# A hybrid decoder step on Trainium2: two of four expert rows fetched whole, row weights ahead of the dots, rows 3 and 2 added first on TensorE

## The reference

```python
def peer_ffn(x, w_pq, sub_keys, u_tab, v_tab):
    B, T, D = x.shape
    nt = B * T
    nb = -(-nt // PEER_BLOCK)
    xf = jnp.pad(x.reshape(nt, D), ((0, nb * PEER_BLOCK - nt), (0, 0))).reshape(nb, PEER_BLOCK, D)

    def one(xb):
        q = (xb @ w_pq).reshape(PEER_BLOCK, PEER_HEADS, 2, PEER_QDIM // 2)
        s = jnp.einsum('phcd,hckd->phck', q, sub_keys).astype(jnp.float32)
        ts, ti = lax.top_k(s, PEER_TOPK)
        cand = ts[:, :, 0, :, None] + ts[:, :, 1, None, :]
        cidx = ti[:, :, 0, :, None] * N_KEYS + ti[:, :, 1, None, :]
        fs, fpos = lax.top_k(cand.reshape(PEER_BLOCK, PEER_HEADS, -1), PEER_TOPK)
        eidx = jnp.take_along_axis(cidx.reshape(PEER_BLOCK, PEER_HEADS, -1), fpos, axis=-1)
        g = jax.nn.softmax(fs, axis=-1)
        u = u_tab[eidx]
        v = v_tab[eidx]
        a = jax.nn.gelu(jnp.einsum('pd,phkd->phk', xb, u).astype(jnp.float32), approximate=False)
        return jnp.einsum('phk,phkd->pd', (g * a).astype(v.dtype), v)

    y = lax.map(one, xf)
    return y.reshape(nb * PEER_BLOCK, D)[:nt].reshape(B, T, D)

def block_tail(x, mix, w_out, ln_g, ln_b, w_pq, sub_keys, u_tab, v_tab):
    h = layer_norm(ALPHA * x + mix @ w_out, ln_g[0], ln_b[0])
    return layer_norm(ALPHA * h + peer_ffn(h, w_pq, sub_keys, u_tab, v_tab), ln_g[1], ln_b[1])
```

## Time and profile before

| | us |
|---|---|
| median of 3 runs | 2192.01 |
| lowest and highest | 2190.14, 2194.75 |
| the profiled execution | 2188.57 |
| its span, first to last instruction | 2186.8 |

### The profile page before, as it was taken

One profiled execution on the slowest core, in us unless ns is written; L12 is line 12 of the kernel. 1 busy time (PEld: TensorE's weight loads), 2 busy tenths in 40 slices (PEclk: granted clock), 3 DMA queues, 4 the chain that ended last, 5 costly groups with the idle time before them and its releaser, 6 DMA issues.

```text
span 2186.8 us, 19928 instructions
## 1 busy us (share of the span) xinstructions
PE 1690.2 (77%) x6362; PEld 997.8 (46%) x6362; DVE 1590.9 (73%) x3268; ACT 474.7 (22%) x1097; POOL 1264.1 (58%) x1129
## 2 busy tenths in 40 slices
PE   7999998993878865859968889699777575585555
PEld 6544666691434432326635656577524232122211
DVE  3532673277878995875789989987787788468775
ACT  1231233112523521211111211111152240011010
POOL 0000000005777787677677777777767777567775
PEclk9999956996988986989989999799898897797777
DMA  4211682336999999999999999999999999999997
GB/s 142 78 69 70 42 251 92 134 132 222 368 366 354 379 320 389 406 377 399 402 409 387 358 376 411 353 405 411 409 405 409 410 404 412 414 376 410 358 387 274
DMA packets 203512, 698.12 MB, mean 319 GB/s; under 512 B 37712, under 2 KB 51728, under 8 KB 194896
## 3 DMA queue, kind: packets, MB, share of 16 engines
q0 software_dynamic: 161504, 604.58, 71.7%
q1 hardware_dynamic: 41904, 92.27, 12.9%
HBM read 690.38 MB, written 10.55 MB: 321 GB/s over the span
## 4 chain that ended last, share of the span: by engine, by line
POOL 33%; PE 28%; DMA 13%; DVE 12%; issue 11%; SPq 2%; ACT 1%; DVEq 0%; ACTq 0%; POOLq 0%
PE bank L823 17%; POOL arena L789 16%; POOL arena L801 15%; PE bank L2139 10%; DMA arena<-in_uv,arena 8%; DVE arena L2040 3%; DMA arena<-in_w_pq 3%; PE bank L835 2%; DVE arena L2058 1%; SPq L2124 1%; DVE arena L1790 1%; POOL arena L768 1%; DVE arena L1787 1%; DMA arena<-in_kwin 1%; SPq L2114 1%
## 5 line engine op out<-in xcount | busy, mean ns | idle before, releaser
L823 PE MATMUL bank<-arena 128*128 128x254 f32 (+15 forms) x4570 | 1314.7, 450 | 437.5 <-DMA arena<-in_uv,arena 294.0
L823 PEld LDWEIGHTS bank<-arena 128*128 128x128 f32 (+5 forms) x4570 | 749.9, 193 | 964.2 <-issue 659.5
L789 POOL DMA_INDIRECT arena<-in_uv,arena x544 | 613.0, 1127 | 374.2 <-DVE arena L1848 177.4
L2040 DVE CUSTOM_DVE_ANT_0 arena<-arena 128x1024 f32<-128x1024 f32 x544 | 649.6, 1226 | 235.3 <-DMA arena<-in_uv,arena 228.0
L801 POOL DMA_INDIRECT arena<-in_uv,arena x544 | 612.7, 1126 | 190.7 <-issue 158.5
L2058 DVE SCALAR_TENSOR_TENSOR arena<-arena 128x1024 f32<-128x1024 f32 x274 | 352.0, 1285 | 42.0 <-DMA arena<-in_uv,arena 32.4
L2139 PE MATMUL bank<-arena 128*128 128x272 f32 (+10 forms) x950 | 267.4, 447 | 13.1 <-DMA arena<-in_xT 8.1
L1654 ACT ACTIVATE arena<-arena 128x128 f32<-128x128 f32 (+1 forms) x265 | 90.8, 389 | 857.5 <-DVE arena L2050 857.3
L2139 PEld LDWEIGHTS bank<-arena 128*128 128x128 f32 (+3 forms) x950 | 153.5, 183 | 123.3 <-issue 91.9
L754 POOL DMA_DIRECT2D arena<-out_p_kc x2 | 1.4, 686 | 328.3 <-DMA out_s_C<-arena 328.3
L1358 ACT ACTIVATE arena<-bank 128x512 f32<-128x512 f32 (+6 forms) x230 | 110.6, 518 | 199.3 <-PE bank L835 163.8
(11 more groups left out here) (244 smaller groups left out, 752.4 us busy)
## 6 DMA issues: line engine op xcount, KB each, us to landing
arena<-in_w_pq SPq DMA_DIRECT2D x10, 2048.0 KB, 10.5
arena<-in_uv,arena POOLq DMA_INDIRECT x1088, 7.9
arena<-in_w_out SPq DMA_DIRECT2D x6, 2048.0 KB, 11.4
arena<-in_w_in SPq DMA_DIRECT2D x5, 2048.0 KB, 7.3
arena<-in_w SPq DMA_DIRECT2D x4, 2048.0 KB, 12.5
arena<-in_w_pq SPq DMA_DIRECT2D x8, 1024.0 KB, 19.6
arena<-in_subk SPq DMA_DIRECT2D x3, 1024.0 KB, 8.6
arena<-in_xT SPq DMA_DIRECT2D x2, 1088.0 KB, 7.9
```

Source lines behind the costliest of these rows:

```text
L789: nc.gpsimd.indirect_dma_start(uv[buf(h, r)][:, 0:D], None, half_rows, bass.IndirectOffsetOnAxis(eidx_u[:, t, s0 + r:s0 + r + 1], 0))\
L823: return te.matmul(out, l, r, start=start, stop=stop)
L2040: last = ve.tensor_tensor_reduce(out=uv[b][:, 0:D], in0=uv[b][:, 0:D], in1=x_sb[:, t, :], scale=1.0, scalar=0.0, op0=ALU.mult, op1=ALU.add ...
```

## The change

Rows 2 and 3 of each half-step are fetched as whole rows of 8 KB, u and v in one gather (`load_uv`, with `WHOLE` = 2 as the first such row); rows 0 and 1 are fetched as before. A half-step has two gathers of u, two of v and two whole ones. The order of issue on GpSimd becomes u(h+1) for rows 0 and 1, v(h) for rows 0 and 1, uv(h+1) for row 3 and then row 2. A whole row waits for the dots of h-1 and for the use of v of the same buffer (`v_row_used`). For whole rows the v half has landed when `s_ur` says so. TensorE takes its rows from 3 downwards, in ScalarE's diagonals as well, and for the first rows of a new tile it waits until the layer norm of the last tile is finished (`s_fin`). `row_weights` is taken out of `weigh_rows`; it stands ahead of the dots of h+1 on VectorE. The retrieval writes the expert numbers doubled for rows 0 and 1 and not doubled for rows 2 and 3.

```diff
--- before.py
+++ after.py
@@ -593,6 +593,8 @@
             t = max(t for t in range(TILES) if H0[t] <= h)
             return t, 4 * (h - H0[t])
 
+        WHOLE = 2
+
         def buf(h, r):
             return 4 * (h % 2) + r
 
@@ -781,23 +783,37 @@
 
             half_rows = i["uv"].rearrange("e (z d) -> (e z) d", z=2)
 
+            def v_row_used(h, r):
+                if r < ND[h]:
+                    pool.wait_ge(s_vf, VSUM[h] + r + 1)
+                else:
+                    pool.wait_ge(s_free, FSUM[h] + 4 - r)
+
+            def load_uv(h):
+                t, s0 = half_slots(h)
+                if h >= 2:
+                    pool.wait_ge(s_dot, h - 1)
+                for r in range(3, WHOLE - 1, -1):
+                    if h >= 2:
+                        v_row_used(h - 2, r)
+                    nc.gpsimd.indirect_dma_start(uv[buf(h, r)], None, i["uv"],
+                                                 bass.IndirectOffsetOnAxis(eidx_u[:, t, s0 + r:s0 + r + 1], 0))\
+                        .then_inc(s_ur[buf(h, r)], 16)
+
             def load_u(h):
                 t, s0 = half_slots(h)
                 if h >= 2:
                     pool.wait_ge(s_dot, h - 1)
-                for r in range(4):
+                for r in range(WHOLE):
                     nc.gpsimd.indirect_dma_start(uv[buf(h, r)][:, 0:D], None, half_rows,
                                                  bass.IndirectOffsetOnAxis(eidx_u[:, t, s0 + r:s0 + r + 1], 0))\
                         .then_inc(s_ur[buf(h, r)], 16)
 
             def load_v(h):
                 t, s0 = half_slots(h)
-                for r in range(4):
+                for r in range(WHOLE):
                     if h >= 2:
-                        if r < ND[h - 2]:
-                            pool.wait_ge(s_vf, VSUM[h - 2] + r + 1)
-                        else:
-                            pool.wait_ge(s_free, FSUM[h - 2] + r - ND[h - 2] + 1)
+                        v_row_used(h - 2, r)
                     nc.gpsimd.indirect_dma_start(uv[buf(h, r)][:, D:2 * D], None, half_rows,
                                                  bass.IndirectOffsetOnAxis(eidx_u[:, t, s0 + r:s0 + r + 1], 0),
                                                  element_offset=D).then_inc(s_vr[buf(h, r)], 16)
@@ -805,6 +821,7 @@
             pool.wait_ge(s_qf, 8)
             pool.wait_ge(s_idx, 1)
             load_u(0)
+            load_uv(0)
             for h in range(N_HALL):
                 if h == 0:
                     pool.wait_ge(s_sf, 8)
@@ -813,6 +830,8 @@
                         pool.wait_ge(s_idx, H0.index(h + 1) + 1)
                     load_u(h + 1)
                 load_v(h)
+                if h + 1 < N_HALL:
+                    load_uv(h + 1)
                 for n in issue.get(h, ()):
                     load_chunk(n)
 
@@ -1319,15 +1338,17 @@
             def first_row(h, r):
 
                 t = half_slots(h)[0]
-                return all(ND[k] == 4 for k in range(H0[t], h)) and r == ND[h]
+                return h == H0[t] and r == 3
 
             def half_rows(h):
                 t, s0 = half_slots(h)
                 M = ROWS[t]
-                for r in range(ND[h], 4):
+                if h in H0[1:]:
+                    pe_eng.wait_ge(s_fin, H0.index(h))
+                for r in range(3, ND[h] - 1, -1):
                     b = buf(h, r)
-                    pe_eng.wait_ge(s_dg, FSUM[h] + r - ND[h] + 1)
-                    pe_eng.wait_ge(s_vr[b], 16 * (h // 2 + 1))
+                    pe_eng.wait_ge(s_dg, FSUM[h] + 4 - r)
+                    pe_eng.wait_ge(s_vr[b] if r < WHOLE else s_ur[b], 16 * (h // 2 + 1))
                     for c2 in range(2):
                         last = mm(PB[c2][0:M, :], diag[b][:, 0:M], uv[b][:, D + c2 * 512:D + c2 * 512 + 512],
                                   first_row(h, r), False)
@@ -1835,7 +1856,10 @@
                         yield
                 link(ve.scalar_tensor_tensor(fa[:, 0, 0:ns], fa[:, 0, 0:ns], float(NK), fa[:, 1, 0:ns],
                                              ALU.mult, ALU.add))
-                link(ve.tensor_scalar(eidx_u[:, t, 0:ns], fa[:, 0, 0:ns], 2.0, None, ALU.mult))
+                by4 = eidx_u[:, t, 0:ns].rearrange("p (k r) -> p k r", r=4)
+                fa4 = fa[:, 0, 0:ns].rearrange("p (k r) -> p k r", r=4)
+                ve.tensor_scalar(by4[:, :, 0:WHOLE], fa4[:, :, 0:WHOLE], 2.0, None, ALU.mult)
+                link(ve.tensor_copy(by4[:, :, WHOLE:4], fa4[:, :, WHOLE:4]))
 
                 link(ve.tensor_copy(gs8[:, 0:nh], fv[:, 0:nh, 0]))
                 ve.tensor_tensor(fv[:, 0:nh], fv[:, 0:nh], gs8[:, 0:nh].unsqueeze(2).to_broadcast([P, nh, TOPK]),
@@ -2042,16 +2066,19 @@
                                                    accum_out=dots[:, b:b + 1])
                 last.then_inc(s_dot, 1)
 
-            def weigh_rows(h):
+            def row_weights(h):
 
                 t, s0 = half_slots(h)
                 h4 = slice(buf(h, 0), buf(h, 0) + 4)
                 dve.wait_ge(s_gl, h + 1)
                 ve.tensor_tensor(w8[:, h4], gel[:, h4], gw[:, t, s0:s0 + 4], ALU.mult).then_inc(s_w8, 1)
                 settle(s_w8)
+
+            def weigh_rows(h):
+
                 for r in range(ND[h]):
                     b = buf(h, r)
-                    dve.wait_ge(s_vr[b], 16 * (h // 2 + 1))
+                    dve.wait_ge(s_vr[b] if r < WHOLE else s_ur[b], 16 * (h // 2 + 1))
                     if h in H0 and r == 0:
                         last = ve.tensor_scalar(acc_v, uv[b][:, D:2 * D], w8[:, b:b + 1], None, ALU.mult)
                     else:
@@ -2065,6 +2092,7 @@
             for h in range(N_HALL):
                 for _ in range(pieces_at(h)):
                     next(todo)
+                row_weights(h)
                 if h + 1 < N_HALL:
                     dot_rows(h + 1)
                 if h in H0[1:]:
```

## The result

The changed kernel took **2389.9 us** in the median of 4 runs (2380.3 to 2393.2), against 2193.0 for the kernel before on the same chip: ratio 1.0928, interval [1.0893, 1.0962]. That is 197 us slower by the two medians and 203 by the ratio, which is not taken from the medians. The forecast was 2213 (2155 to 2270): the sign was right, the size wrong by a factor of more than nine. The profiled execution took 2393.2 us, span 2391.3, against a span of 2186.8 before: 204.5 us to be found.

A forecast was written before the change was run, and what follows sets the result against it. GpSimd's issuing was taken to bound three stretches, with the DMA engines near their bound in 1028 to 1845 us. +50 - 12 - 4 - 4 - 9 - 4 + 8 - 4 = +21 on 2188.6, plus 3.4 to the median: 2213 us (2155 to 2270).

The forecast's parts named there:

- Step (4): Where VectorE adds one or two rows: whole-row fetches wait for TensorE, two half-steps take 20 to 21 us; +8 us (0 to 25).
- heavier coupling: Rival: L is 7.2, half-steps lose 0.5 us each as TensorE frees rows late, gains halved; +94, 2286 us, chance 0.13.
- Step (3): Half-steps 69 to 108: row 2's fetch stands open behind VectorE's third addition, period 13.1 against 12.25 us; +50 us (+4 to +80).
- L: Time from a whole row's issue on GpSimd to its landing; 5.5 or 6.5 us, taken as 6.5.
- The estimate from the Trainium skill's page: Gather priced at 2.0 us plus bytes over 436 GB/s: landing 5.4 us after issue, the open fetch +25, the sum 25 us lower.
- Step (1): Six gathers a half-step, not eight, relieve GpSimd: gains 12 us in 540 to 780, 4 in 780 to 850, 4 and 9 later.
- this stretch's rate would rise above 390 GB/s: Sign to look for in 540 to 780 us: DMA rate above 390 GB/s, against 367; otherwise GpSimd was not its bound.
- Step (2): Same bytes in larger packets: 0.6% of the 817 us of the third and fourth stretches, gain 4 us (0 to 10).
- the change doesn't do what it says: Rival: an 8 KB row could move as two 4 KB packets, taking back 4 us and changing no sign; no chance given.
- Step (5): Weights ahead of the dots on VectorE: TensorE can start a half-step earlier; new norm wait costs nothing; no term in the sum.
- Step (6): End of the kernel: no v rows have to land after the last dots; gain 4 us (0 to 8).

The follow-up runs named there:

- experiment 1: Changed kernel with no whole rows (all u and v in halves, 8 gathers a half-step), its reorderings kept: 2188.3 us, 1.0024 against the kernel before.
- experiment 12: Changed kernel with no whole-row wait for TensorE or VectorE (constants replace v of rows 2 and 3), each whole row moved as two halves: 2233.8 us, 1.0219.
- experiment 3: Changed kernel with TensorE and VectorE using constants for v of rows 2 and 3, so whole rows wait for the dots alone: 2195.7 us, 1.0047.
- 2: Changed kernel with TensorE using a constant for v of rows 2 and 3, so whole-row gathers don't wait for TensorE: 2249.3 us, 1.0302.
- experiment 5: Changed kernel with VectorE adding two rows, not three, in half-steps 69 to 108, row 2 going to TensorE: 2357.3 us, 1.0778.
- experiment 8: Changed kernel with each whole row's gather replaced by two gathers of 4 KB rows behind the same waits: 2456.1 us, 1.1233.

## Why the prediction was wrong in size

Going down the experiments, the loss is: reorderings +5 us (1), later dots and changed order of fetches +43 (12 against 1), fewer issues and larger packets -38 (3 against 12), wait for VectorE's third addition +56 (2 against 3), wait for TensorE +137 (changed against 2). The sum is 203 us, as it must be, since the terms are the steps of one chain of kernels. Each term holds for its place in the chain; another order of steps would share the loss out in another way.

**Step (4) failed, the wait for TensorE.** It had the right loop over two half-steps, but "up to 9 us until TensorE has used them" was 12.8 us in the mean with the issue (half-steps 3 to 27) and 17.7 in the round shown, and the pair took 10.9 us in the mean where the step had 9.0. So the two half-steps took 26.1 us, not 20 to 21. This was the term: 8 us, with an end of 25, for what measured 137. The prediction named the sign of it, GpSimd waiting for TensorE, and that is what came (436 us). Three things were left out of the 9 us. The pieces of VectorE, ScalarE and TensorE lie one behind the other, not side by side: 8.0 us of VectorE until the weights, then 9 us of ScalarE and TensorE. TensorE's pieces themselves wait for VectorE's. And in that round its clock is at the lower level. The times of the diagonals in the earlier trace rows should have been read against the end of the dots in an ordinary half-step, and not only in a cluster. The sentence that the wait "costs nothing while these pieces last under some 9 us" was never held against a row.

The rival "heavier coupling" had the right mechanism at the wrong price: 0.5 us for each of 68 half-steps. It was 1.1 us for each of 133 (144 us by the table), in 2 to 27 most of all, 1.7 each, where TensorE takes three of the four rows. Its 68 half-steps also leave out 109 to 134, where TensorE uses both whole rows and the wait measured 19 us.

**Step (3) held.** +50 forecast, 56 in the runs and 52 in its stretch; L was 6.5 in the forecast, and 5.48, 5.65 and 7.68 us in the rounds shown. The estimate from the Trainium skill's page "DMA: Bandwidth & Descriptors" (section Anatomy of one DMA) was 5.4. The trace agrees for gathers that find the queues empty (5.5 us for the one at 752.82, and 5.4 is the least in the trace), not for the loop (a median of 8.0). What the step did not see is that in the real kernel TensorE's wait is in the same stretch and covers about half of this price (28 us come back in experiment 5).

**Step (1), the relief of GpSimd,** has its size in the sum and not in its places. 12 + 4 us were forecast for 540 to 850, and experiment 3 has 16 us less than experiment 1 there; but experiment 12, with as many issues as experiment 1, already has 7 of them, so 9 are left for the issues and packets, and that 16 met 16 is luck. The 7 come with the order of the fetches, by a way that no run parts. The 4 and 9 us of the later stretches are not there in 3 against 1 (+5 in half-steps 43 to 68, 0 in 109 to 134), and are 2 and 2 in 3 against 12. The forecast that this stretch's rate would rise above 390 GB/s was wrong: 323 in the changed kernel, 377 even in experiment 3.

**Step (2)** can't be told apart from (1); the two together are 38 us against 33. An 8 KB row is one packet: those under 8 KB fell by 73,984, the 69,632 forecast and 16 small ones for each of the 272 issues that went. So the rival that the change doesn't do what it says is out.

**Step (5)** held, nearly: it counted nothing for the reorderings, and experiment 1 has 5 us, with 10 as the end. It was right to see what row weights ahead of the dots are for, but the step counted only VectorE's side of TensorE's start. **Step (6)** held: from the end of the last dots to the end of the span 20.6 us against 23.3, 2.7 less.

**Missing altogether:** that dots which need a whole row start later. At the start it is 7 us, and it is the likeliest reading of most of the 43 us in experiment 12, which is argued and not shown. What the lower mean clock (0.82 against 0.87) adds, as TensorE idles more, was not measured by itself either: TensorE's busy time rose by 71 us, and how much of that lay in the loop is open.

The sign is not all luck. Without TensorE's wait and the later dots, the terms measured are +5 + 56 - 38 = +23 us, where the forecast without its +8 for step (4) was +13. In the prediction's sum two small slips change nothing: 32 half-steps from 11.3 to 12.1 us are 24 us and not 26, and 0.6% of 817 us is 5 and not 4.

## What to carry to other kernels

When two transfers become one, the new one waits for the last user of either half. Before pricing that, walk one ordinary round of the loop in the trace, engine by engine, from the end of the first use to the release of the buffer by the last. A release that today is hidden by two rounds may be half again as late as its own work suggests, and twice as late in some rounds (12.8 and 17.7 us here for the 9 assumed), since pieces on three engines stand one behind the other.

An engine's shorter busy time is worth what the next bound leaves of it: here 314 us less of GpSimd gave 9 us in the first stretch that it bounds and 38 us in all, and fewer issues with larger packets gave the most (67 us) only where they stood in a loop.

Two waits in one stretch can cover each other: VectorE's was worth 52 us with TensorE's gone, and 28 with it there. Take away both, and each alone.

## What the runs showed of the hardware

One gather with 8 KB in a partition needs the same time of GpSimd as one with 4 KB (0.94 us and 0.30 us to the next), and twice the bytes. With 2 GB/s in the queues ahead of it, 1 MB landed 5.5 us after its issue at 752.82; the least of the changed kernel is 5.4 us, against 4.0 us as the least for the 0.5 MB gathers of experiment 8.

TensorE's granted clock was at 1.00 up to 741.2 us and at 0.50 from there to 751.4, over the end of a wait of 4.76 us (737.96 to 742.72), while its matmuls were what GpSimd, the queues and VectorE all waited for. So in this round the engine that was late ran slower while it was the bound. In the mean of half-steps 2 to 27 its clock was 0.82, against 0.87 before.
